# A hybrid SSD and mixture-of-experts layer on one core: modulation products at other steps of VectorE's order, the first scan output loaded over two freed input chunks, expert weights loaded once per run of blocks

## What is computed

```python
mx = modulation(c, ada_w, ada_b)             # silu(c) @ ada_w (2048 x 12288) + bias, split in 6
hx = modulate(rms_norm(x, norm_g[0]), mx[0], mx[1]);  hc = the same for ctx
# SSD mixer: z, x, B, C, dt = h @ w_in; depthwise convolution, silu; scans in both directions
yx = rms_norm(y_lat * silu(z), ssm_norm_g) @ ssm_w_out
x  = x + mx[2] * yx
hx = modulate(rms_norm(x, norm_g[1]), mx[3], mx[4])
# mixture of experts: top-1 of 4 groups, top-2 of its 8 experts; 32 experts, 512 assignments
y  = sum over the chosen experts of gate * ((silu(t @ w_gate[e]) * (t @ w_up[e])) @ w_down[e])
out = x + mx[5] * y
```

## Time and profile before

| | |
|---|---|
| three runs, us | 2176.36, 2176.81, 2181.66 (median 2176.81) |
| profiled execution, us | 2174.73 |
| its span, first to last instruction, us | 2173.2 |
| busy, us (share of the span) | PE 1974.7 (91%), DVE 1229.5 (57%), ACT 498.0 (23%), POOL 153.9 (7%) |
| data moved | 666.68 MB, mean 307 GB/s |
| mean clock granted to PE | 0.96 of full |

### The profile page before, as it was taken

The page is one execution under the profiler, slowest core; times in us unless marked ns, Lnnn a source line. Parts: engine busy times, 40 slices in busy tenths (PEclk is TensorE's granted clock), DMA queues, the critical chain, the costliest instruction groups (busy, mean ns, idle before and its releaser), DMA issues.

```text
span 2173.2 us, 27626 instructions
## 1 busy us (share of the span) xinstructions
PE 1974.7 (91%) x10090; PEld 1222.7 (56%) x10090; DVE 1229.5 (57%) x1999; ACT 498.0 (23%) x577; POOL 153.9 (7%) x214
## 2 busy tenths in 40 slices
PE   5778999999999999989988899888989889999888
PEld 2368887878888887867877533333333333333332
DVE  2457898888888888887875533133323223332224
ACT  3232434333333342434444200000000000000000
POOL 0000010100000000000881000000000000000000
PEclk9789999999999999999999999999999999999999
DMA  9958676767676767678754699999999999999996
GB/s 354 319 163 265 182 234 174 239 177 240 181 224 202 216 195 229 196 229 284 268 181 161 272 426 425 427 425 426 428 426 426 427 425 427 428 426 426 427 425 268
DMA packets 294718, 666.68 MB, mean 307 GB/s; under 512 B 13505, under 2 KB 188001, under 8 KB 261009
## 3 DMA queue, kind: packets, MB, share of 16 engines
q1 hardware_dynamic: 285728, 639.45, 78.7%
q0 software_dynamic: 7984, 26.40, 3.6%
q10 hardware_dynamic: 960, 0.23, 0.1%
HBM read 655.40 MB, written 10.65 MB: 306 GB/s over the span
## 4 chain that ended last, share of the span: by engine, by line
DMA 29%; PE 17%; POOL 4%; DVE 1%; issue 1%; SPq 1%; ACT 0%; DVEq 0%; POOLq 0%
DMA wt<-in_moe_w_up 29%; PE bank L1849 12%; PE bank L1706 2%; POOL ysq L640 1%; POOL ysq L647 1%; POOL ysq L645 1%; PE bank L1874 1%; SPq L531 1%; PE bank L1813 0%; PE bank L1814 0%; PE bank L1831 0%; PE bank L1765 0%; PE bank L1758 0%; PE bank L1806 0%; DVE x L1483 0%
## 5 line engine op out<-in xcount | busy, mean ns | idle before, releaser
L1849 PE MATMUL bank<-wt,xe 128*64 128x512 f32 x1984 | 468.0, 627 | 82.3 <-DMA wt<-in_moe_w_up 82.3
L1483 DVE TENSOR_TENSOR x<-x,bank 128x512 f32<-128x512 f32 x256 | 158.5, 682 | 538.1 <-PE bank L1831 538.1
L1603 PE MATMUL bank<-hTh,whi 128*128 128x256 f32 (+1 forms) x1264 | 413.7, 347 | 8.5 <-ACT whi L708 5.9
L1604 PE MATMUL bank<-hTl,whi 128*128 128x256 f32 (+1 forms) x1264 | 407.2, 342 | 0.0
L1849 PEld LDWEIGHTS bank<-wt,xe 128*64 128x64 f32 x1984 | 164.8, 144 | 382.5 <-issue 382.5
L1603 PEld LDWEIGHTS bank<-hTh,whi 128*128 128x128 f32 x1264 | 245.8, 194 | 37.7 <-issue 6.1
L1604 PEld LDWEIGHTS bank<-hTl,whi 128*128 128x128 f32 x1264 | 245.9, 195 | 25.5
L1608 PE MATMUL bank<-hTh,wlo 128*128 128x256 f32 (+1 forms) x1264 | 231.2, 335 | 0.2 <-DVE wlo L959 0.2
L1874 PE MATMUL bank<-wt,hdn 128*64 128x512 f32 x1024 | 226.8, 595 | 1.4 <-DVE hdn L1495 1.4
L871 ACT ACTIVATE gsb<-bank 128x512 f32<-128x512 f32 x32 | 19.1, 597 | 838.0 <-PE bank L1849 838.0
L1608 PEld LDWEIGHTS bank<-hTh,wlo 128*128 128x128 f32 x1264 | 196.8, 190 | 24.7 <-DVE wlo L959 0.4
(11 more groups left out here) (304 smaller groups left out, 1836.0 us busy)
## 6 DMA issues: line engine op xcount, KB each, us to landing
wt<-in_moe_w_gate SPq DMA_DIRECT2D x64, 2048.0 KB, 16.6
wt<-in_moe_w_up SPq DMA_DIRECT2D x64, 2048.0 KB, 21.1
wt<-in_moe_w_down SPq DMA_DIRECT2D x64, 2048.0 KB, 18.5
raw<-in_ssm_w_in SPq DMA_DIRECT2D x80, 1024.0 KB, 5.8
raw<-in_ada_w SPq DMA_DIRECT2D x70, 1024.0 KB, 6.1
raw<-in_ssm_w_out SPq DMA_DIRECT2D x32, 1024.0 KB, 5.1
fr<-in_ada_w SPq DMA_DIRECT2D x26, 1024.0 KB, 11.3
bc<-cum_d POOLq DMA_DIRECT2D x32, 512.0 KB, 5.3
```

Of the source, the lines that this page charges most:

```text
L1483: dve.tensor_tensor(x1[:, tt, cols], x1[:, tt, cols], banks[(1, 3, 6, 7)[nb]][:, :], ALU.add).then_inc(s_acc2, 1)
L1603: pe.matmul(bank[:, 0:width], wh[:, k, :], hTh[:, k, 0:width], start=(k == 0), stop=False)
L1604: last = pe.matmul(bank[:, 0:width], wh[:, k, :], hTl[:, k, 0:width], start=False, stop=False)
L1849: last = pe.matmul(banks[0][SLOTS * h:SLOTS * h + SLOTS, :], rows[:, k, :], wt[2 * q + h][:, FF * i:FF * i + FF], start=(k == 0), stop=(k ...
```

## The change

**Modulation products.** In a group with projections, tile 6 moves from behind the drain of step 8 to ahead of it, and tile 7 from step 9, ahead of its drain, to step 8, behind its drain. Nothing else on DVE moves in the loop. **First scan output.** The two loads of group 0 no longer wait for the end of the last projection's two halves but for the end of its products with k = 0 and 1 in each half (`s_kfree`), and SP issues them ahead of the third `w_out` tile instead of behind it. **Expert weights.** A run is the blocks of one expert. The table gets three more rows (first block of a run less one, run of a block, number of runs), 64 columns per row instead of 128; SP loops over runs and waits for the last block of the run before; PE reads the run of its block from the table at the head of each block and waits for that run's loads. DVE makes the new columns, PE turns six columns instead of three.

```diff
-ADA_STEP = {1: 1, 2: 2, 5: 3, 6: 4, 7: 5, 8: 6, 9: 7}
+ADA_BEFORE = {5: 3, 8: 6}
+ADA_AFTER = {1: 1, 2: 2, 6: 4, 7: 5, 8: 7}
+TAB = 64
...
@@ SP, output projection
             for i, (nb, q) in enumerate(OTILES):
+                if i == RAW - 1:
+                    sp.wait_ge(s_kfree, 1)
+                    y_load(0, 0)
+                    sp.wait_ge(s_kfree, 2)
+                    y_load(0, 1)
...
                 if i == RAW - 1:
-                    sp.wait_ge(s_wh, M_OUT)
-                    y_load(0, 0)
                     sp.wait_ge(s_win, M_OUT)
-                    y_load(0, 1)
@@ SP, experts
-            with sp.Fori(1, nblk) as b:
-                e = sp.value_load(itab[0:1, bass.ds(b, 1)], min_val=0, max_val=NE - 1)
+            nrun = sp.value_load(itab[0:1, 5 * TAB:5 * TAB + 1], min_val=2, max_val=NE)
+            with sp.Fori(1, nrun) as r:
+                e = sp.value_load(itab[0:1, bass.ds(r, 1)], min_val=0, max_val=NE - 1)
+                last = sp.value_load(itab[0:1, bass.ds(r + 3 * TAB, 1)], min_val=0, max_val=TAB)
                 for j in range(2 * NQ):
-                    sp.wait_ge(s_gu[j % 2], b * NQ + (j // 2 + 1 - NQ))
+                    sp.wait_ge(s_gu[j % 2], last * NQ + (j // 2 + 1))
                     up_gate(bass.ds(e, 1), j)
@@ DVE, groups
-                    if w and n in (5, 9):
-                        ada_sum(g, ADA_STEP[n])
+                    if w and n in ADA_BEFORE:
+                        ada_sum(g, ADA_BEFORE[n])
                     if w and n != 4 and not (isinstance(g, int) and g == 0 and n == 0):
                         drain(g, n)
...
-                    if w and n in (1, 2, 6, 7, 8):
-                        ada_sum(g, ADA_STEP[n])
+                    if w and n in ADA_AFTER:
+                        ada_sum(g, ADA_AFTER[n])
@@ DVE, table of blocks (one of the new columns)
+            ch(dve.tensor_scalar(rs[:, RUN, :], rs[:, NB, :], 0.0, None, ALU.is_gt))
+            ch(dve.tensor_tensor_scan(rs[:, REND, :], rs[:, T0, :], rs[:, RUN, :], 0.0, ALU.mult, ALU.add))
+            ch(dve.tensor_tensor(rs[:, RBEG, :], rs[:, REND, :], rs[:, RUN, :], ALU.subtract))
@@ PE, last projection
+                final = isinstance(m, int) and m == M_OUT - 1
...
+                    if final and k == 1:
+                        last.then_inc(s_kfree, 1)
@@ PE, experts
-                    for i in range(3):
-                        last = pe.matmul(banks[3][0:1, P * i:P * i + P], rs[:, 7, i:i + 1], ident[:, :], start=True, stop=True)
+                    for i, col in enumerate((0, 1, 2, 5, 6, 7)):
+                        last = pe.matmul(banks[3][0:1, TAB * i:TAB * i + TAB], rs[:, 7, col:col + 1], ident[:, 0:TAB], start=True, stop=True)
...
+                    run = pe.value_load(itab[0:1, bass.ds(b + 4 * TAB, 1)], min_val=0, max_val=NE - 1)
                     pe.wait_ge(s_xe, b)
...
-                    pe.wait_ge(s_wt[2 * q], b * 16 + 16)
-                    pe.wait_ge(s_wt[2 * q + 1], b * 16 + 16)
+                    pe.wait_ge(s_wt[2 * q], run * 16 + 16)
+                    pe.wait_ge(s_wt[2 * q + 1], run * 16 + 16)
```

More of the change, by code:

```diff
@@ L234, in build @@
         pick = at("pick", 186, [P, TT, 3, NE])
-        rs = at("rs", 184, [P, 12, NE])
+        rs = at("rs", 184, [P, 16, NE])
         ridx = at("ridx", 187, [P, TT, 2, 8], U32)
@@ L252, in build @@
         slot = at("slot", 193.5, [P, P])
-        itab = at("itab", 188, [1, 3 * P], I32)
+        itab = at("itab", 188, [1, 6 * TAB], I32)
         hdn = at("hdn", 190, [P, FC, SLOTS])
@@ L293, in build @@
         s_wh = sem("s_wh")
+        s_kfree = sem("s_kfree")
         s_drain = sem("s_drain")
@@ L563, in _ @@
                     for h in range(2):
-                        sp.wait_ge(s_dn[h], b * FC + (2 * w + 2 - FC))
+                        sp.wait_ge(s_dn[h], last * FC + (2 * w + 2))
                     down(bass.ds(e, 1), w)
@@ L865, in _ @@
             act.wait_ge(s_tab, 1)
-            nblk = act.value_load(itab[0:1, 2 * P:2 * P + 1], min_val=2, max_val=P)
+            nblk = act.value_load(itab[0:1, 2 * TAB:2 * TAB + 1], min_val=2, max_val=TAB)
             def expert(b):
@@ L1330, in done @@
                 dve.wait_ge(s_v, chained[0])
-            CNT, START, NB, BEND, BBEG, OH, OFF, COL, T0, LAST = range(10)
+            CNT, START, NB, BEND, BBEG, OH, OFF, COL, T0, LAST, RUN, REND, RBEG, ROH, BRUN = range(15)
             dve.wait_ge(s_rprep, 3)
@@ L1420, in _ @@
             done()
+            inc(dve.scalar_tensor_tensor(rs[:, ROH, :], rs[:, REND, :], pidx[:, 0:1], rs[:, ROH, :], ALU.is_gt, ALU.mult))
             ch(dve.scalar_tensor_tensor(rs[:, OH, :], rs[:, BEND, :], pidx[:, 0:1], rs[:, OH, :], ALU.is_gt, ALU.mult))
+            inc(dve.tensor_tensor(rs[:, BRUN, :], rs[:, OH, :], rs[:, RBEG, :], ALU.mult))
+            inc(dve.tensor_tensor(rs[:, RUN, :], rs[:, ROH, :], rs[:, BBEG, :], ALU.mult))
+            inc(dve.tensor_tensor(rs[:, ROH, :], rs[:, ROH, :], iota_e[:, :], ALU.mult))
             inc(dve.tensor_tensor(rs[:, OFF, :], rs[:, OFF, :], rs[:, OH, :], ALU.mult))
@@ L1424, in _ @@
             done()
-            ch(dve.tensor_tensor(rs[:, OH, :], rs[:, OH, :], iota_e[:, :], ALU.mult))
-            inc(dve.tensor_reduce(rs[:, COL, 0:1], rs[:, OH, :], AX_X, ALU.add))
+            inc(dve.tensor_reduce(rs[:, COL, 0:1], rs[:, ROH, :], AX_X, ALU.add))
+            inc(dve.tensor_reduce(rs[:, COL, 5:6], rs[:, RUN, :], AX_X, ALU.add))
+            inc(dve.tensor_reduce(rs[:, COL, 6:7], rs[:, BRUN, :], AX_X, ALU.add))
+            inc(dve.tensor_copy(rs[:, COL, 7:8], rs[:, REND, NE - 1:NE]))
             inc(dve.tensor_reduce(rs[:, COL, 3:4], rs[:, OFF, :], AX_X, ALU.add))
@@ L1429, in _ @@
             done()
+            inc(dve.tensor_scalar(rs[:, COL, 5:6], rs[:, COL, 5:6], -1.0, 0.0, ALU.add, ALU.max))
             ch(dve.scalar_tensor_tensor(rs[:, COL, 1:2], pidx[:, 0:1], float(SLOTS), rs[:, COL, 3:4], ALU.mult, ALU.add))
@@ L1488, in expert @@
                 first = isinstance(b, int)
-                after = dve.value_load(itab[0:1, bass.ds(b + (P + 1), 1)], min_val=0, max_val=ROWS)
+                after = dve.value_load(itab[0:1, bass.ds(b + (TAB + 1), 1)], min_val=0, max_val=ROWS)
                 if not first:
@@ L1837, in expert @@
                 if first:
+                    run = 0
                     pe.wait_ge(s_xgA, KC)
@@ L1870, in expert @@
                 for f in range(FC):
-                    pe.wait_ge(s_wt[2 * NQ + f // 2], b * 16 + 16)
+                    pe.wait_ge(s_wt[2 * NQ + f // 2], run * 16 + 16)
                     for nb in range(4):
```

9 lines of the change are left out of this document (5 added, 4 removed).

## The result

| | before | after |
|---|---|---|
| median of four runs beside each other, us | 2177.10 (2176.36 to 2181.66) | 2126.39 (2125.82 to 2130.66) |
| profiled execution, us | 2174.73 | 2125.82 |
| its span, us | 2173.2 | 2124.3 |

The ratio is 0.9766 with a 95% interval of 0.9754 to 0.9779: 2.3% faster, 50.7 us by the medians and 48.9 us by the profiled spans. Predicted were 47.5 us and 2129 us.

What follows compares the result with a forecast made beforehand. PE was taken to bound the group loop and the DMA engines the experts' stage; 29.9 + 7.7 + 9.9 = 47.5 us off the profiled 2174.7 gave 2127, predicted 2129 as median, range 2119 to 2146.

Steps and rivals of the forecast that it cites:

- Modulation tiles: Group loop: moving tiles 6 and 7 removes PE's waits for DVE's `arow`, 19.8 us, plus half clock behind, 10.1: 29.9.
- the count of six: Group loop: six of seven waits of about 3.3 us have 1.7 us of half clock behind them, 10.1 us.
- Rivals 1 and 4: Group loop: saved time returns at other waits, 2149 (0.14); clock dips stay, 2139 (0.18 shared by three rivals).
- First scan output: End of last projection: earlier `yl` load starts first output tile sooner, bounds 3.5 and 11.8, middle taken, 7.7 us.
- a row that the prediction had named as a sign of being wrong: PE's list of waits: a new row of PE waiting for `wlo` or `cv` would show the forecast wrong.
- Rival 3: First output tile: PE can't use the early load, held by ACT and DVE, 2133 us; 0.18 shared by three rivals.
- Expert weights: Experts' stage: one set of six tile loads saved, a 19.0 us pause in place of 29.5, gain 10.5 us.
- The pause: Experts' stage: transfers stop while PE uses the kept tiles for the expert's second block, 19.0 us.
- rival 2: Experts' stage: all blocks are of different experts, 32 runs, so no gain, 2139 us; 0.18 shared by three rivals.
- Table: Ahead of first expert block: DVE's added instructions and PE's doubled transposes delay it and all transfers, 0.6 us.
- PE's register load: Head of each expert block: 0.49 us, 31 times, hidden in 0.88 + 2.70 us of waiting for weights, costing nothing.
- Rival 5: Experts' stage: each register load drains PE's queue; at 6 us per load the time is 2203 us; chance 0.02.

Runs made afterwards that it cites:

- the filled wait: Kernel before, with thirteen matmuls of constants added per group ahead of PE's wait for tile 7, tiles not moved: 2169.23 us, ratio 0.9945.

## Why the prediction was right, point by point

- **Modulation tiles: 29.9 predicted, 31.8 measured.** Each step held: the wait is gone in every group, DVE's drains and `wlo` are not late, and the clock stays up. Of 31.8 us, 19.8 are the seven waits and 10.1 the half clock behind six of them: the granted clock is 0.72 in the 6 us behind each of these six, and 1.00 behind the first group's wait of 0.41 us. So the count of six was right, and the filled wait shows that this share is real. The last 1.9 us the prediction didn't have: 0.4 of them stood ahead of the first group's wait already, the rest is some 0.2 a group. Rivals 1 and 4 fell.
- **First scan output: 7.7 predicted, 7.9 measured, but most of it isn't the load's, and that the two agree is luck.** The term named the load as the cause. The tiles alone give 7.0 of it, the load alone 5.6, and the load on top of the tiles 0.9 to 1.7. The prediction had the reason in its own text (SP stands on DVE's last tile until 969.04) and put the saving on the wrong part. Its middle between 3.5 and 11.8 was a choice and not a chain; the limit is DVE and ACT, as the three small waits show, and the idle time of 6.5 us turned into 3.5 us of waiting for them. One of the three, 1.1 us for `cv`, is a row that the prediction had named as a sign of being wrong; it stands at this boundary alone, and none came inside a group. Rival 3, that PE can't use the early load, is nearly right as to the load.
- **Expert weights: 10.5 predicted, 9.5 measured from the first block on; with the table 9.9 and 9.3.** The pause is mis-sized: 20 us and not 19.0. Its first block ran 1.6 us longer at half clock behind its 2.72 us wait, a dip that the prediction's 7.09 from a block without one left out; the register load, set at 0.5, cost nothing. There were 31 runs, as worked out, so rival 2 fell.
- **Table: 0.6 predicted, at most 0.2 measured.**
- **PE's register load.** Free, as predicted, but for another reason. The prediction hid it in the wait for weights. It is hidden first in the 3.9 us by which the sequencer is ahead (in the changed kernel's trace one load starts at 1407.5, while the products ahead of it last until 1411.5), and only then in those waits. The row in the changed kernel (ns, shortest, median, longest) is below the 0.49 us of the earlier trace rows, which was a single one:

```profile
L1866 PEldq TENSOR_LOAD <-itab x31: 297/302/317, 1205.6 to 2077.1; - x31
```

The Trainium skill, "DMA: Bandwidth & Descriptors", section "Latency and other measured facts", gives a floor of about 600 ns. The record alone, 0.30, is half of that; the distance from load to load, 0.645, is near it. Rival 5 (slower) was a matter of size: with 12 more loads, 8.4 us a block, it happens.

What stays open is why the kernel before has no single time. Its loop over groups ended at 969.07 us in its own profile, and the unchanged copy of it in three of the experiments at 973.78, 974.70 and 977.02. The waits were 23.3 us there and 25.5, 24.3 and 26.4 here; most of the rest is half clock. The 10 us behind the second group's wait, in the kernel before and in the kernel with runs only (columns as in the earlier trace rows):

```profile
333.00:343.00 10.00, 8.79 (x36) 7.26 (x37) 9.41 (x26) 1.30 (x2) 0.00 (x0) 0.83 0.83 235
333.00:343.00 10.00, 9.03 (x30) 7.57 (x31) 8.73 (x25) 0.46 (x1) 0.00 (x0) 0.66 0.84 241
```

A granted clock of 0.83 is 1.7 us lost, and 0.66 is 3.4. Behind the six waits it was 0.83 each time in the kernel before; in the kernel with the early load alone it was 0.66 three times, with runs only four times (once 0.69). What decides between the two I did not find. In all nine profiles of kernels with moved tiles the loop ended between 933.7 and 935.1. So the move is worth 5 to 8 us more against such executions than against the profiled one, on which the prediction was built. The 5 us by which the tiles-only kernel exceeded its traces fit that; it isn't shown, since no execution of the kernel before was profiled beside it.

## What to carry to other kernels

A wait of some 3 us on the bounding engine cost what it lasted and then half as much again in clock, or as much; filling it with idle products recovered that second part, removing it recovered both. Before crediting an edit with a gain at a boundary, ask which other edit ends the same wait: here two parts gave 7.0 and 5.6 us alone and 7.9 together. When one buffer per tile is kept for a second use, the stream pauses for two thirds of a block, so loading once saved a third of what the loads took.

## What the runs showed of the hardware

- PE's sequencer was some 4 us ahead of the array (3.9 and 4.0 in two traces): nine register reads at 0.645 us, 5.8 us in all, left a gap of 2.1.
- The half clock behind a gap is not one price: gaps of 4.7 us cost 1.5 and 2.7 us in turn. With gaps of 2.1 us five of the eleven blocks that start between 1300 and 1650 us took 15.7 us for 64 products that take 13.9, the others ran them at full clock. Behind waits of 3.0 to 4.1 us in the loop it cost 1.7 or 3.4 us.
- POOL's small products slow down by half beside a busy DVE, 0.72 to 1.06 us (`ysq` of L648). The Trainium skill, "GPSIMD Engine Reference", section "Specifications", lists its access to SBUF as shared with VectorE, with contention where that one has two inputs in SBUF; the instruction on DVE here is of that kind, and the trace agrees.
